# Eight experts in order of their token counts, as one straight program with slots for 128 and 64 tokens in turn

## The reference, cut to what matters

```python
TOP_K = 2
N_EXP = 8
E_FF = 3584
'o_router': nrm((NO, D, N_EXP), inv(D)),
'o_moe_w_in': nrm((NO, N_EXP, D, 2 * E_FF), inv(D)),
'o_moe_w_out': nrm((NO, N_EXP, E_FF, D), inv(E_FF)),
```

## Time and profile before

| | |
|---|---|
| runs, median (lowest to highest) | 2319.2 us (2318.0 to 2321.45), 3 runs |
| profiled execution: its span, from first to last instruction | 2312.3 us |
| profiled execution: its own time | not given beside the span; the runs' median lies 6.9 us above the span |
| granted TensorE clock, mean (1 is full speed) | 0.943 |
| moved by DMA in the span | 492.38 MB |

### The profile page before, as it was taken

One profiled execution on the slowest core, in us unless ns is written; L12 is line 12 of the kernel. 1 busy time (PEld: TensorE's weight loads), 2 busy tenths in 40 slices (PEclk: granted clock), 3 DMA queues, 4 the chain that ended last, 5 costly groups with the idle time before them and its releaser, 6 DMA issues. The chain is left out here.

```text
span 2312.3 us, 27555 instructions
## 1 busy us (share of the span) xinstructions
PE 2050.3 (89%) x11534; PEld 1435.5 (62%) x11535; DVE 614.1 (27%) x1261; ACT 326.0 (14%) x610; POOL 41.1 (2%) x65
## 2 busy tenths in 40 slices
PE   5997897789999898788888979997979998998997
PEld 3876887687888687777766534454534454444443
DVE  4436566542000354566622000001000001000002
ACT  1012222210000133222211100010000010000001
POOL 0001000000000000000000000000000000000000
PEclk8998998899999999889897999999999999999998
DMA  8739211102443341300014997789997789876760
GB/s 325 286 123 426 108 74 74 74 9 109 149 159 129 155 146 37 151 10 10 10 46 197 428 358 286 291 361 425 427 407 291 287 323 426 334 285 255 285 223 19
DMA packets 37093, 492.38 MB, mean 213 GB/s; under 512 B 4380, under 2 KB 4541, under 8 KB 7325
## 3 DMA queue, kind: packets, MB, share of 16 engines
q1 hardware_dynamic: 36956, 490.33, 54.0%
HBM read 487.95 MB, written 2.36 MB: 212 GB/s over the span
## 5 line engine op out<-in xcount | busy, mean ns | idle before, releaser
L2009 PE MATMUL bank<-ring,arena 128*128 128x512 f32 x896 | 399.7, 601 | 39.5 <-issue 39.5
L2009 PEld LDWEIGHTS bank<-ring,arena 128*128 128x128 f32 x896 | 169.9, 193 | 240.3 <-issue 240.3
L2083 DVE TENSOR_TENSOR arena<-bank,arena 128x256 f32<-128x256 f32 (+1 forms) x56 | 31.3, 559 | 866.3 <-PE bank L2009 565.0
L2005 PE MATMUL bank<-ring,arena 128*64 128x256 f32 x1792 | 210.5, 391 | 22.8 <-issue 22.6
L2025 PE MATMUL bank<-ring,arena 128*128 128x512 f32 x448 | 197.3, 593 | 2.7 <-ACT arena L1981 2.7
L2005 PEld LDWEIGHTS bank<-ring,arena 128*64 128x64 f32 x1792 | 129.5, 140 | 94.9 <-issue 39.2
L1231 PE MATMUL bank<-arena,ring 128*128 128x256 f32 x704 | 155.3, 383 | 4.0 <-DVE arena L292 3.8
L2025 PEld LDWEIGHTS bank<-ring,arena 128*128 128x128 f32 x448 | 84.9, 190 | 108.8 <-issue 105.1
L1231 PEld LDWEIGHTS bank<-arena,ring 128*128 128x128 f32 x704 | 134.1, 192 | 24.4 <-issue 4.1
L1352 PE MATMUL bank<-arena,ring 128*128 128x256 f32 x512 | 115.6, 388 | 6.4 <-DVE arena L292 3.8
L701 PE MATMUL bank<-arena 128*128 128x128 f32 x768 | 102.5, 289 | 14.0 <-issue 9.9
(11 more groups left out here) (346 smaller groups left out, 1982.6 us busy)
## 6 DMA issues: line engine op xcount, KB each, us to landing
ring<-in_experts SPq DMA_DIRECT2D x168, 2048.0 KB, 10.1
ring<-in_stream SPq DMA_DIRECT2D x61, 2048.0 KB, 11.8
arena<-in_masks SPq DMA_DIRECT2D x1, 1280.0 KB, 5.8
xT<-in_xT SPq DMA_DIRECT2D x1, 1024.0 KB, 6.8
arena<-in_s0gd SPq DMA_DIRECT2D x4, 256.0 KB, 3.3
out_sgd<-arena SPq DMA_DIRECT2D x4, 256.0 KB, 2.5
out_y<-arena SPq DMA_DIRECT2D x4, 256.0 KB, 2.5
arena<-in_hfw SPq DMA_DIRECT2D x1, 544.0 KB
```

Source lines behind the costliest of these rows:

```text
L2005: mm = nc.tensor.matmul(out[HALF * c:HALF * c + HALF, 0:256], hA[:, j, 0:HALF], w[:, j, 256 * c:256 * c + 256], start=(j == 0), stop=(j == ...
L2009: mm = nc.tensor.matmul(out[:], hA[:, j, :], w[:, j, :], start=(j == 0), stop=(j == DC - 1))
L2083: V.tensor_tensor(actb[:, k % 2, 0:n], ps[2 * (k % 2) + 1][:, 0:n], sgl[:, k % 2, 0:n], ALU.mult)\
```

## The change

Experts are taken in the order of their counts, four from the upper half and four from the lower half in turn, with room for 128 and 64 tokens in turn (`MAIN_CAPS`). The order is found on the chip: VectorE ranks the counts (`tokr`), makes a permutation of it (`perm`) and from that the list of experts (`order`), the permuted slots (`pos`) and weights (`wgt`); `over` is now set if some expert has more tokens than its place has room. The body of an expert is written out 8 times with the size that its place has, so there is no loop and no branch on `few`; semaphores are compared with constants. SP reads the number of the expert of each place into a register and loads its tiles. The products of one expert run on into the next: `hA` has two halves, the next expert's tokens are gathered in steps 5 and 6 of the one before, and the result of an expert is copied, scattered (one quarter in each of the steps 1 to 4, all into bank 5) and added during the next one. A pass with 128 slots for each expert stands ahead of this one in every engine's program and runs only if `over` is set. `feed` ends with the tiles of the fixed layers. Gathering no longer stands in the block of the routing.

The diff, cut:

```diff
         def feed(sp, upto):
 
-            while feed.n < min(upto + RING, STREAM_TILES + EXP_TILES * NE):
+            while feed.n < min(upto + RING, STREAM_TILES):
                 n = feed.n
                 if n >= RING:
                     sp.wait_ge(s_used, n - RING + 1)
-                src = A["stream"][n] if n < STREAM_TILES else A["experts"][(n - STREAM_TILES) // EXP_TILES,
-                                                                           (n - STREAM_TILES) % EXP_TILES]
-                sp.dma_start(slot(n), src).then_inc(s_slot[n % RING], 16)
+                sp.dma_start(slot(n), A["stream"][n]).then_inc(s_slot[n % RING], 16)
                 feed.n += 1
         feed.n = 0
...
 
         drop(NCONST[2])
         yg7 = take(GH, TT)
         hT = take(DC, TT)
...
+        hA = take(2, DC, T)
         moe = take(DC, TT)
-        m_route = floats[0]
...
                 pe.wait_ge(s_cnt7, 1)
+                nc.tensor.matmul(ps[5][:, 0:8], ones, sel[:, 0, :], start=True, stop=False)
+                nc.tensor.matmul(ps[5][:, 0:8], ones, sel[:, 1, :], start=False, stop=True).then_inc(s_rk, 1)
                 nc.tensor.matmul(ps[7][:, 0:8], cc("tri_sb"), sel[:, 0, :], start=True, stop=True)
                 nc.tensor.matmul(ps[7][:, 8:16], cc("tri_sb"), sel[:, 1, :], start=True, stop=False)
-                nc.tensor.matmul(ps[7][:, 8:16], ones, sel[:, 0, :], start=False, stop=True)
-                nc.tensor.matmul(ps[7][:, 16:24], ones, sel[:, 0, :], start=True, stop=False)
-                nc.tensor.matmul(ps[7][:, 16:24], ones, sel[:, 1, :], start=False, stop=True).then_inc(s_rk, 1)
-                pe.wait_ge(s_htc, 4)
-                pe.wait_ge(s_P, 1)
-                pe_gather(pe, 0)
-                pe.wait_ge(s_hB, 1)
-                pe_gather(pe, 1)
+                nc.tensor.matmul(ps[7][:, 8:16], ones, sel[:, 0, :], start=False, stop=True).then_inc(s_rk, 1)
...
+                for q in range(NE):
+                    dve_link.last(dve, V.memset(caps[:, q:q + 1], float(MAIN_CAPS[q])))
...
+                dve.wait_ge(s_rk, 1)
+                dve_link(dve, V.tensor_copy(tok, ps[5][:, 0:8]))
+                dve_link.last(dve, V.tensor_tensor(picks[0], rows(tok), tok.unsqueeze(2).broadcast_to([P, NE, NE]), ALU.is_gt))
+                dve_link(dve, V.tensor_tensor(picks[1], rows(tok), tok.unsqueeze(2).broadcast_to([P, NE, NE]), ALU.is_equal))
+                dve_link(dve, V.tensor_tensor(picks[1], picks[1], tie, ALU.mult))
+                dve_link(dve, V.tensor_tensor(flat8(picks[0]), flat8(picks[0]), flat8(picks[1]), ALU.add))
+                dve_link(dve, V.tensor_reduce(tokr, picks[0], AX.X, ALU.add))
+
+                for h in range(2):
+                    dve_link.last(dve, V.tensor_tensor(perm[:, h:NE:2, :], tokr.unsqueeze(1).broadcast_to([P, NE // 2, NE]),
+                                                       cc("iota")[:, 4 * h:4 * h + 4].unsqueeze(2).broadcast_to([P, NE // 2, NE]),
+                                                       ALU.is_equal))
                 dve_link.sync(dve)
-                V.tensor_scalar(sel, cnt, 1.5, None, ALU.is_lt).then_inc(s_cnt7, 1)
-                dve_link.last(dve, V.tensor_tensor(top, s1[:, 0], L, ALU.mult))
-                dve_link.last(dve, V.tensor_tensor(wd, s1[:, 1], L, ALU.mult))
+                dve_link(dve, V.tensor_tensor(tmp8, perm, rows(cc("iota")[:, 0:NE]), ALU.mult))
+                dve_link(dve, V.tensor_reduce(toks, tmp8, AX.X, ALU.add))
+                V.tensor_scalar(order, toks, 0.0, None, ALU.add).then_inc(s_plan, 1)
+
+                dve_link(dve, V.tensor_tensor(picks[0], perm, rows(tok), ALU.mult))
+                dve_link(dve, V.tensor_reduce(tokr, picks[0], AX.X, ALU.add))
+                dve_link(dve, V.tensor_tensor(tokr, tokr, caps, ALU.subtract))
+                dve_link(dve, V.tensor_reduce(most[:, 0:1], tokr, AX.X, ALU.max))
+                V.tensor_scalar(over, most[:, 0:1], 0.0, None, ALU.is_gt).then_inc(s_plan, 1)
...
-        def rounds(eng, expert, after=lambda it: None):
-            def body(it):
-                some = eng.value_load(few[0:1, bass.ds(it, 1)], min_val=0, max_val=1)
-                with eng.If(some > 0):
-                    expert(it, True)
-                with eng.If(some < 1):
-                    expert(it, False)
-                after(it)
-
-            with eng.Fori(0, NE) as it:
-                body(it)
-            eng.wait_ge(s_flag, 1)
-            more = eng.value_load(over[0:1, 0:1], min_val=0, max_val=1)
-            with eng.If(more > 0):
-                with eng.Fori(NE, 2 * NE) as it:
-                    body(it)
+        class Pass:
+
+            def __init__(self, caps, pos, at, base, slot, used, signals):
+                self.caps, self.pos, self.at, self.base, self.slot, self.used = caps, pos, at, base, slot, used
+                (self.P, self.Pw, self.gat, self.hA, self.sil, self.act, self.tr, self.aT, self.Ct, self.C, self.ye, self.sc,
+                 self.acc) = signals
+
...
+            def arrived(self, eng, n):
+                m = self.at + n
+                eng.wait_ge(self.slot[m % RING], self.base + 16 * (m // RING + 1))
+
+            def consumed(self, eng, n):
+                eng.wait_ge(self.used, self.base + self.at + n + 1)
...
+        gate_at = lambda i: 3 * i - 1 if i else 0
+        up_at = lambda i: gate_at(i) + 1
+        out_at = lambda i: 3 * i + 4 if i < STEPS - 1 else 3 * STEPS - 1
...
+        def sp_pass(sp, m):
+
+            def load(n, e, t):
+                p = m.at + n
+                if n >= RING or m.at:
+                    sp.wait_ge(m.used, m.base + p - RING + 1)
+                sp.dma_start(m.tile(n), A["experts"][bass.ds(e, 1), t].rearrange("a p c -> (a p) c"))\
+                    .then_inc(m.slot[p % RING], 16)
+
+            before = None
+            for i in range(STEPS):
+                q, k = divmod(i, KC)
+                if k == 0:
+                    e = sp.value_load(order[0:1, q:q + 1], min_val=0, max_val=NE - 1)
+                g = 3 * k - 1 if k else 0
+                load(gate_at(i), e, g)
+                load(up_at(i), e, g + 1)
+                if i:
+                    load(out_at(i - 1), e if k else before, 3 * k + 1 if k else EXP_TILES - 1)
+                before = e
+            load(out_at(STEPS - 1), e, EXP_TILES - 1)
...
+            def gather(q, half):
+                c = m.caps[q]
+                for j in range(4 * half, 4 * half + 4):
+                    for s in range(NS):
+                        mm = nc.tensor.matmul(ps[5][:, (j % 4) * T:(j % 4) * T + c], htok[:, s, j * P:(j + 1) * P], Psel[:, s, 0:c],
+                                              start=(s == 0), stop=(s == 1))
+                mm.then_inc(m.gat, 1)
...
+            for i in range(STEPS):
+                q, k = divmod(i, KC)
+                if k == 0:
+                    pe.wait_ge(m.hA, m.base + 2 * q + 2)
+                if i >= 2:
+                    pe.wait_ge(m.act, m.base + i - 1)
+                in_product(i, gate_at(i), ps[2 * (i % 2)])
+                if i:
+                    transposes(i - 1)
+                if k == 0 and q:
+                    weights(q - 1)
+                if 1 <= k <= 4 and q:
+                    if k == 1:
+                        pe.wait_ge(m.C, m.base + q)
+                        pe.wait_ge(m.ye, m.base + q)
+                    else:
+                        pe.wait_ge(m.acc, m.base + 4 * (q - 1) + k - 1)
+                    scatter(q - 1, k - 1, ps[5])
+                if k >= 5 and q < NE - 1:
+                    if k == 5:
+                        pe.wait_ge(m.P, m.base + q + 2)
+                        if q:
+                            pe.wait_ge(m.acc, m.base + 4 * q)
+                    else:
+                        pe.wait_ge(m.hA, m.base + 2 * q + 3)
+                    gather(q + 1, k - 5)
+                if i == STEPS - 1:
+                    pe.wait_ge(m.acc, m.base + 4 * q)
+                    weights(q)
+                in_product(i, up_at(i), ps[2 * (i % 2) + 1])
+                if i:
+                    project(i - 1)
+            transposes(STEPS - 1)
+            project(STEPS - 1)
+            pe.wait_ge(m.act, m.base + STEPS)
+            pe.wait_ge(m.aT, m.base + STEPS)
+            pe.wait_ge(m.C, m.base + NE)
+            pe.wait_ge(m.ye, m.base + NE)
+            for b in range(4):
+                scatter(NE - 1, b, ps[BANKS[b]])
...
+            def result(q):
+                c = m.caps[q]
+                m.consumed(act, out_at(KC * q + KC - 1))
+                if q:
+                    act.wait_ge(m.sc, m.base + 4 * q)
+                for h in range(2):
+                    o = 512 * h
+                    if c == HALF:
+                        ins = nc.scalar.activation(ye[0:HALF, o:o + 512], ps[6][HALF * h:HALF * h + HALF, :], ACT.Copy)
+                        continue
...
```

(55 more changed lines are left out.)

394 lines of the change are left out of this document (175 added, 219 removed).

## The result

| | before | after |
|---|---|---|
| median of 3 runs, us | 2319.2 | 2234.97 (2228.06 to 2235.18) |
| ratio, 95% interval | | 0.9629 [0.9613, 0.9644] |
| profiled execution: span, us | 2312.3 | 2226.3 |
| first expert product, us from the span's start | 1242.3 | 1247.55 |
| expert stage: first expert product to the end of the last scatter, us | 1049.6 | 959.5 |

The changed kernel is faster by 84.2 us in the medians and by 86.0 us in the two profiled spans.

A forecast was written before the change was run, and what follows sets the result against it. The expert stage was taken as bound by TensorE, with a seam of 4 to 12 us behind each expert. Removing 87.6 us and adding 9.1 took the span from 2312.3 to 2233.8, the median to 2240.7 us; range 2226 to 2262.

The forecast's parts named there:

- Seams: Between experts: TensorE's "issue" pauses, put down to branches on registers, go in the straight program; 58.9 us won.
- cold starts: An expert's first three tiles, slower behind a pause, run at normal speed except in the first expert; 11.3 us won.
- Tails: At an expert's end: TensorE's waits for copies hide under the next expert's products, except in the last; 10.6 us won.
- Tile waits: In the second of two neighbouring small experts: three waits for weights go, as wide experts refill the ring; 3.2 us won.
- Gathers: Behind the last expert: gathers for a nonexistent ninth go, 3.6 us; narrower gathers for small experts might save up to 7.
- The start: Ahead of the first expert: loads wait for the order and a jump over the second pass; first product 9.1 us later.
- Weights set the pace: In small experts: TensorE waits for weight tiles because loads are slower than products; priced at 2260 us, chance 0.10.
- Seven tiles land together: At the stage's start: DMA engines share the first seven loads, so the first lands late; total 2266 us, chance 0.06.
- Late code: Throughout the straight program: TensorE waits for code in each of 56 steps; 2577 us at 6.0 us each, chance 0.04.
- It does more: Behind the overflow flag: if set, eight more wide experts run, bringing the total beyond 3400 us; chance 0.01.
- New waits between the engines: In the expert stage: the won time comes back as waits between engines, total near 2319 us; chance 0.02.

The follow-up runs named there:

- e9_drain_far: e3_drain with two far jumps, over 300 never-executed products each, added behind the scatter at each of seven seams; 2326.62 us, ratio 1.0039.
- r0_again: The changed kernel run once more, unaltered, as the base for the other runs; 2231.95 us, ratio 0.9639.
- e3_drain: Changed kernel with the overlap between neighbouring experts taken back: each expert ends, scatter included, before the next one's first product; 2249.24 us, ratio 0.9706.
- e7_inorder: Changed kernel with experts taken by number, without ranking (small, wide, small, small, wide, small, wide, wide), sizes fixed to that; 2267.79 us, ratio 0.9792.
- e2_grouped: Changed kernel with the four wide experts first and then the four small ones, instead of in turn; 2281.42 us, ratio 0.9847.
- e1_far: Changed kernel with one TensorE jump over 300 never-executed products ahead of each expert but the first; 2242.15 us, ratio 0.9669.
- e5_mid: Changed kernel with three of four wide experts given 96 places, as 12 products of 128 columns a slice instead of one of 512; 2293.93 us, ratio 0.9896.

## Why the prediction was right, term by term

Its sum for the profiled execution was 2233.8 us, measured 2226.3: 7.5 less. 3.9 of these are the start, 2.5 the stage (959.5 against 962.0) and 1.1 the end, where VectorE's reads of the loop's flags (2292.7 to 2294.1 us in the kernel before) are gone, which the sum had not counted.

- **Seams (58.9) and cold starts (11.3).** Gone, shown by the missing lines and, from the other side, by e9_drain_far. There were seven seams and not eight: the eighth pause is the 3.25 us ahead of the first expert, as the sum has it. What the prediction did not see is that a branch costs only what it lasts beyond the queued work: one far jump at each seam of the pipelined program left TensorE standing for 8.1 of 32.5 us. What pipelining alone would have won, with the loop's branches left in, was not tried. The first expert kept 0.23 us of cold start (20.84 - 3 x 6.87) and not 1.84, but in this execution only: in r0_again, where the granted clock was 0.50 up to the first product, it kept 2.19, near the forecast.
- **Tails (10.6).** Right: 1.9 us left of 11.8 where 1.2 were forecast, and e3_drain brings 11.4 back.
- **Tile waits (3.2).** Right, and the order is their reason: e7_inorder and e2_grouped, 31.4 and 49.3 us of waits.
- **Gathers (3.6 for the ninth, up to 7 for the narrow ones).** The ninth is gone; a gather into 64 slots takes 1.73 us, one into 128 1.79: as good as nothing saved.
- **The start (+9.1).** The mechanism was right, two sizes were off. The block ended at 1234.5 (forecast 1234.9; VectorE's 35 operations took exactly the 7.0 us). The jump over the second pass took 3.3 us and not 6.0, and the tile landed 7.8 us after its issue and not 8.6. The first product started at 1247.55 and not at 1251.4: +5.2. The mis-sized term is the jump: it was priced by branches that ran beside full loads, and this one ran ahead of the first expert load (TensorE's own: 3.4 us). The far jumps of e1_far bear out that the loads make the difference: 3.3 to 3.8 us beside half-loaded DMA engines, 6.1 to 6.3 beside full ones. TensorE's own path was forecast to end 2.2 us ahead of the tile, with gathers and copies of 7.1 us. It ended 1.1 us ahead here (6.9 us, to 1246.44), and in r0_again it ended last (8.9 us at the lower clock): the two paths are level, and that the tile came last, as forecast, is partly luck. The Trainium skill's estimate of 6.8 us for the tile (page "DMA: Bandwidth & Descriptors", "Anatomy of one DMA") is 1.0 short of the trace.
- **The rivals.** *Weights set the pace* was refuted for this order, and shown for two others; the 358 GB/s that the Trainium skill (the same page, "Where 436 GB/s comes from") gives as the bound for loads from HBM is passed again, with one core at work, by the 428 GB/s of the window from 1247. *Seven tiles land together* was refuted: the first landed 7.83 us after its issue, the next 4.9 behind it. *Late code* did not happen here and is real in e5_mid. *It does more* did not: 168 expert tiles were loaded, eight times 21. *New waits between the engines* did not come: 1.9 us, in the last expert.

**Open:** three executions of the changed kernel had spans of 2226.3, 2233.5 and 2233.3 us; what makes the 7 us was not found.

## What to carry to other kernels

A far branch costs what it lasts beyond the work that is queued when the sequencer reaches it, and it lasts longer beside full loads; so count the queued work at the place first. A drained pipeline leaves less of it, and its short pauses can bring the lower clock back. When a stage is made gapless, its loads become the next bound: count the lead of the ring in issue-to-landing time, and place work that is slower than its loads between work that is faster. Smaller products pay only while code arrives faster than they use it up.

## What was unexpected of the hardware

- Straight-line code arrived at about 256 instructions (16 KB) per 6.1 us beside full expert loads, and TensorE waited for it (113.4 us in e5_mid).
- A jump over 300 products took 3.3 to 3.8 us beside half-loaded DMA engines and 6.1 to 6.3 beside full ones, since the 16 KB of code came 2.6 us later, and over ten products 0.2 us; queued work hid three quarters of it in e1_far.
- With pauses of up to 1.4 us the granted clock fell to half at three seams of e3_drain and stayed at 1.00 at four.
- Products on four groups of 32 columns overlap (5.45 us a tile), but those on groups of 64 and of 32 in turn did not (0.94 us a slice, where the two alone add up to 0.68).
